# TensorE's order inside each turn of a chunked RWKV recurrence: the next block's inverse step put ahead of the state chain's step

## The chip, the cores and the metric

The kernel runs on one core of one Trainium2 chip. The metric is the device time of one execution in microseconds (us). The kernel before was timed three times: median 4484.01 us, from 4480.31 to 4486.97. The execution that left the profile took 4483.24 us.

A core has a matrix engine (TensorE, PE in the rows, its weight loads PEld), VectorE (DVE), ScalarE (ACT) and GpSimd (POOL), each with its own instruction queue which it works off in order, and SyncE (SP), which here issues the DMAs. They synchronise by semaphores. Matmuls write to PSUM, which has 8 banks; all operands here are float32.

## The reference

The program is three transformer blocks in sequence on 512 tokens of width 1024. The change touches one branch of the last layer, a bidirectional RWKV-7 recurrence with 16 heads of 64 channels:

```
def wkv7_step(state, inp):
    r, w, k, v, a, b = inp
    sa = jnp.einsum('...ij,...j->...i', state, a)
    state = (state * w[..., None, :] + sa[..., :, None] * b[..., None, :]
             + v[..., :, None] * k[..., None, :])
    y = jnp.einsum('...ij,...j->...i', state, r)
    return state, y
```

It is scanned over the 512 tokens forwards and backwards, with `-kk` (the normalised keys) as a and `kk * a` as b. Everything else (two FFNs, a gated delta rule, attention, an SSD and an HGRN scan, a second even layer, a Fourier branch) runs before or after this stage and is not touched.

## The kernel before

The scan is done in chunks. Two heads and one direction make one of 16 items i (ft = i // 2 is the pair of heads, d = i % 2 the direction), and the 512 tokens of an item are 4 chunks of 128. Within a chunk the recurrence becomes a triangular system: its inverse is built first (for all 4 chunks and both heads of the item at once, by doubling the block size from 2 to 64), and then the state is carried through the 4 chunks in sequence.

Four kinds of work are written as Python generators, for each engine one: `head` and `body` (what makes the decayed operands, the score matrices and their masks), `inverse` and `chain` (the state through the chunks); every second item there is also a `tail` (the normalisation of the output). `rw_rounds` (L401) runs 17 rounds r = -1..15. In round r an engine works at the chain of item r, the inverse of item r + 1, the body of item r + 2, the head of item r + 3 and, in even rounds, the tail of item r - 1. `together` (L205) takes one step (up to the next `yield`) of each generator in the order in which they are given, and starts again: one such pass is called a turn here. So the order of an engine's instructions within a turn is the order of the streams in the call of `together`, and nothing else reorders them. A round has some 14 turns; `chain` has three steps for each chunk n = 0..3, in turns 3n, 3n + 1 and 3n + 2.

What the steps issue on TensorE, with what they wait for:

- chain, turn 3n (n > 0): L3732, old state times keys ("rw rhs"); needs `rw s in`, VectorE's L3834 of the turn before.
- chain, turn 3n + 1: L3746, the inverse times the right side ("rw u", 4 small products, recorded as 8); needs VectorE's L3812 (which adds the own part to rhs).
- chain, turn 3n + 2: L3754 (own part of the state's update), L3756 (the update's part by the negated u; needs VectorE's L3817, which negates u, or for n = 0 ScalarE's L3786), L3762 (old state into the output) and L3764 (negated u into the output). VectorE then scales and adds the state (L3827, for n = 0 L3829) and masks it for the next chunk (L3834).
- inverse, even turns from 2: L938 ("inv x", 16 products), from turn 4 on also four transposes L923 ("inv t"); odd turns from 3: L954 ("inv y", 16 products). Turn 1 is four transposes L923 ("inv d"). x needs what VectorE's L1055 made of the y before, y needs what L1046 made of the x before and, from turn 5, ScalarE's copy L1010 of the transposes; the first x needs ScalarE's copy L1005 of turn 1.
- body and head: the scores L3459 (turns 3, 6, 8, 10), which VectorE masks in L3611, transposes L3442, L3428 (turn 5), L3374 (turn 0), L3499 and L3502.

VectorE's order within a turn is chain, inverse, body, head, tail, as it is on TensorE and ScalarE. PSUM banks are taken in turn from 7 (the eighth holds the chain's output), so an instruction may also wait until the tile that had its bank 7 takes before has been read.

Of the kernel before, what the change touches and what calls it, by code (L numbers as in the profile page):

```python
# [15 lines left out]
NT = 4  # L16
# [164 lines left out]
def run(steps):  # L181
    for _ in steps:
        pass
# [15 lines left out]
def behind(turns, steps):  # L199
    for _ in range(turns):  # L200
        yield
    yield from steps


def together(*streams):  # L205
    streams = list(streams)
    while streams:
        streams = [g for g in streams if next(g, "end") != "end"]
        yield
# [20 lines left out]
def assemble(nc, ctx, io, out):  # L230
# [25 lines left out]
    PS = [ctx.enter_context(nc.psum_tensor(f"ps{i}", [128, 512], F32))[:, :] for i in range(8)]  # L256
    banks, weights, sets = Turns(8), Turns(4), Turns(2)

    def mem(at_, tiles, width=TOK):
        return View(main[:, at_:at_ + tiles * width].rearrange("p (a b) -> p a b", b=width))  # L260
# [642 lines left out]
    def part128(a, i):  # L903
        return a[:, i * 128:(i + 1) * 128]
# [1182 lines left out]
    def ssd_order(d):  # L2087
        return list(range(NT)) if d == 0 else list(range(NT - 1, -1, -1))
# [1249 lines left out]
    RS_S, RS_S1 = mem(7232, 1, 128)(0), mem(7360, 2, 128)  # L3338
# [62 lines left out]
    def rw_rounds(e, head, body, inverse, chain, tail, aside):  # L3401


        none = iter(())
        run(together(rw_rest[e.name], behind(2, head(e, 1))))
        for r in range(-1, 16):
            ends = tail(e, r - 1) if r > 0 and r % 2 == 0 else none
            own = behind(0, chain(e, r)) if r >= 0 else none
            whole = inverse(e, r + 1) if r < 15 else none
            feeds = body(e, r + 2) if r < 14 else aside(e, r)  # L3410
            ahead = behind(5, head(e, r + 3)) if r < 13 else none
            run(together(*((own, whole, feeds, ahead, ends) if e.name == "act" else (own, whole, feeds, ahead, ends))))
        run(tail(e, 15))
        e.fence("rwkv")

# [302 lines left out]
    def pe_rw_chain(pe, i):  # L3718
        s, ft, d = sem["pe", "rwkv"], i // 2, i % 2
        FM, VK, MS, DT, RP = FMs[i % 3], VKs[i % 3], MSs[i % 6], DTs[i % 3], RPs[i % 3]  # L3720
        yb, before_y = banks.take("rw y", i, among=(0,))
        for hd in range(2):
            pe.wait_ge(*at("out", "rw ms", i, 4 * hd + 3))
        for n, c in enumerate(ssd_order(d)):
            s_ = slice(c * 128, (c + 1) * 128)
            rhs = RP[:, s_]
            if n:
                b, before = banks.take("rw rhs", i, n)
                if before:
                    pe.wait_ge(*at("out", *before))  # L3730
                pe.wait_ge(*at("rw s in", i, n))
                pe.mm(PS[b][:, 0:128], FM(0)[:, s_], RS_S1(n % 2), start=True, stop=True).then_inc(  # L3732
                    pe.inc(s, "mm", "rw rhs", i, n), 1)
                rhs = RS(0)
            yield
            b, before = banks.take("rw u", i, n)
            if before:
                pe.wait_ge(*at("out", *before))
            pe.wait_ge(*(at("out", "rw rhs", i, n) if n else at("out", "rw rhs own", i)))
            pe.wait_ge(*at("out", "inv t", 64, "early", "rw", i))  # L3740
            for k in range(2):
                pe.wait_ge(*at("out", "inv y", 64, k, "rw", i))
            pe.wait_ge(*at("rw dt zero", i))
            for hd in range(2):
                for h in HALF:
                    t = pe.mm(PS[b][h, 64 * hd:64 * hd + 64], part128(DT(hd), c)[:, h], rhs[:, 64 * hd:64 * hd + 64],  # L3746
                              start=True, stop=True)
            t.then_inc(pe.inc(s, "mm", "rw u", i, n), 1)
            yield
            if n < NT - 1:  # L3750
                b, before = banks.take("rw ds", i, n)
                if before:
                    pe.wait_ge(*at("out", *before))
                pe.mm(PS[b][:, 0:128], VK(1)[:, s_], VK(0)[:, s_], start=True, stop=False)  # L3754
                pe.wait_ge(*at("out", "rw u", i, n))
                pe.mm(PS[b][:, 0:128], VK(2)[:, s_], RS(1), start=False, stop=True).then_inc(  # L3756
                    pe.inc(s, "mm", "rw ds", i, n), 1)
            pe.wait_ge(*at("out", "rw u", i, n))
            if n == 0 and before_y:
                pe.wait_ge(*at("out", *before_y))  # L3760
            if n:
                pe.mm(PS[yb][:, s_], RS_S1(n % 2), FM(1)[:, s_], start=False, stop=False)  # L3762
            for hd in range(2):
                t = pe.mm(PS[yb][H2[hd], s_], RS(1)[:, 64 * hd:64 * hd + 64], MS[hd](3)[:, s_], start=n == 0,  # L3764
                          stop=n == NT - 1)
            t.then_inc(pe.inc(s, "mm", "rw y", i, n), 1)
            yield
# [138 lines left out]
    def pe_rwkv(pe):  # L3906
        input_here("lora")
        banks.only(range(1, 8))
        rw_rounds(pe, pe_rw_head, pe_rw_body, pe_rw_inverse, pe_rw_chain, pe_rw_tail, pe_rw_aside)
        banks.only(range(8))  # L3910

    def act_rwkv(a):
        after(a, "p")
        rw_rounds(a, act_rw_head, act_rw_body, act_rw_inverse, act_rw_chain, act_rw_tail, act_rw_aside)
# [14 lines left out]
    def dve_rwkv(v):  # L3929
        after(v, "p")  # L3930
        rw_rounds(v, dve_rw_head, dve_rw_body, dve_rw_inverse, dve_rw_chain, dve_rw_tail, dve_rw_aside)
# [203 lines left out]
```

## Time and profile before

| | |
|---|---|
| median of 3 runs | 4484.01 us |
| profiled execution, its own time | 4483.24 us |
| its span, first to last instruction | 4481.4 us |
| TensorE busy | 4331.1 us (97%) |
| VectorE busy | 2717.4 us (61%) |
| ScalarE, GpSimd busy | 793.4 us (18%), 171.5 us (4%) |
| mean granted TensorE clock | 0.990 |
| rounds 0 to 12 of the recurrence | 3745.7 to 4198.1 us |

Busy time is what the engine's instructions took, matmuls with their modelled ends, so 97% says that TensorE has few gaps and not that each of its cycles does work. The recurrence begins in the span at some 3717 us (round -1) and its chain ends at 4304 us. A round that has a tail is longer than one that has none. The granted clock is given as a share of 2.4 GHz, so 0.50 is the lower of the clock's two levels, 1.2 GHz. The time outside the span is 4483.24 - 4481.4 = 1.84 us.

### The profile page before, as it was taken

The page shows a single profiled execution, that of the slowest core. Times are in us where ns is not written, and L with a number is a line of the kernel's source. Part 1 is how long each engine was busy: PE and PEld are TensorE (multiplying, and loading weights), DVE is VectorE, ACT ScalarE, POOL GpSimd, SP SyncE. Part 2 cuts the span into 40 slices and gives each one's busy share as a digit, 9 for nine tenths or more (in the row PEclk, how much of TensorE's full clock was granted, in tenths as well). Part 3 has the DMA queues.
Part 4 walks back from the last instruction along what each step waited for, and adds up shares of the span by engine and source line. Part 5 has one row for each costly group of instructions (what it writes and reads, how often), then busy time and mean ns, then how long its engine had stood idle before and what let it go on. Part 6 is the DMA issues. An engine that isn't in the chain of part 4 may idle for free.

```text
span 4481.4 us, 68176 instructions
## 1 busy us (share of the span) xinstructions
PE 4331.1 (97%) x29692; PEld 3361.7 (75%) x29692; DVE 2717.4 (61%) x4765; ACT 793.4 (18%) x1434; POOL 171.5 (4%) x281
## 2 busy tenths in 40 slices
PE   9999999999999999999999999999999998999899
PEld 7887445577887888876755678887888787777767
DVE  6675878355555446676444556566556548888736
ACT  0001012221022000221222210000100104444311
POOL 0000000010000000000000000000000003222100
PEclk9999999999999999999999999999999999999999
DMA  7533454103222222111210122222222210000031
GB/s 256 169 115 64 68 75 69 29 2 85 94 94 66 94 85 87 59 57 38 66 48 29 55 69 93 85 85 76 94 73 88 81 47 12 2 3 3 12 103 48
DMA packets 284378, 311.52 MB, mean 70 GB/s; under 512 B 5168, under 2 KB 277936, under 8 KB 281008
## 3 DMA queue, kind: packets, MB, share of 16 engines
q1 hardware_dynamic: 284080, 307.16, 24.2%
q8 instruction: 234, 3.83, 0.4%
q14 instruction: 64, 0.52, 0.0%
HBM read 305.04 MB, written 2.10 MB: 69 GB/s over the span
## 4 chain that ended last, share of the span: by engine, by line
PE 90%; DVE 6%; ACT 2%; issue 1%; DMA 0%; SPq 0%; DVEq 0%; POOL 0%; ACTq 0%; POOLq 0%
PE ps L399 50%; PE ps L323 18%; PE ps L368 2%; PE ps L3459 1%; PE ps L2703 1%; PE ps L2489 1%; PE ps L938 1%; PE ps L923 1%; PE ps L954 1%; PE ps L540 1%; PE ps L2169 1%; PE ps L2158 1%; PE ps L3362 1%; PE ps L1383 1%; PE ps L754 0%
## 5 line engine op out<-in xcount | busy, mean ns | idle before, releaser
L399 PE MATMUL ps<-main 128*128 128x256 f32 x5888 | 1305.7, 379 | 0.0
L399 PEld LDWEIGHTS ps<-main 128*128 128x128 f32 x5888 | 1119.8, 190 | 151.0
L399 PE MATMUL ps<-main,w 128*128 128x256 f32 x4436 | 992.7, 380 | 3.5 <-DVE main L472 1.8
L399 PEld LDWEIGHTS ps<-main,w 128*128 128x128 f32 x4436 | 844.4, 191 | 122.9 <-issue 7.5
L323 PE MATMUL ps<-main,w 128*128 128x512 f32 (+1 forms) x1952 | 843.6, 587 | 12.7 <-DMA main<-in_xT 7.6
L323 PEld LDWEIGHTS ps<-main,w 128*128 128x128 f32 x1952 | 370.0, 193 | 423.7 <-issue 409.7
L491 DVE TENSOR_TENSOR main<-main,ps 128x512 f32<-128x512 f32 x189 | 130.0, 688 | 455.3 <-PE ps L399 454.9
L488 DVE TENSOR_TENSOR main<-main,ps 128x512 f32<-128x512 f32 x123 | 84.4, 686 | 233.8 <-PE ps L399 231.0
L438 ACT COPY main<-ps 128x256 f32<-128x256 f32 x123 | 45.7, 371 | 964.8 <-PE ps L399 962.4
L764 DVE SCALAR_TENSOR_TENSOR main<-main,params_sb 128x512 f32<-128x512 f32 x256 | 192.5, 752 | 9.1
L496 DVE TENSOR_TENSOR main<-main,ps 128x512 f32<-128x512 f32 x189 | 130.0, 688 | 86.9 <-PE ps L399 84.4
L448 DVE TENSOR_TENSOR main<-w 128x512 f32<-128x512 f32 (+2 forms) x189 | 127.6, 675 | 45.2 <-DMA w<-in_o_w_in 11.7
L451 DVE TENSOR_TENSOR main<-main,w 128x512 f32<-128x512 f32 (+2 forms) x189 | 128.9, 682 | 6.6
L453 DVE TENSOR_TENSOR main<-w,main 128x512 f32<-128x512 f32 (+2 forms) x189 | 128.9, 682 | 6.4
L449 DVE TENSOR_TENSOR main<-w 128x512 f32<-128x512 f32 (+2 forms) x189 | 127.6, 675 | 0.0
L3688 POOL MEMSET w<- 128x512 f32 x128 | 60.6, 525 | 1577.1 <-DVE tmp L3638 1282.6
L2544 DVE TENSOR_TENSOR main<-main 128x512 f32<-128x512 f32 x56 | 38.8, 692 | 127.7 <-PE ps L2489 125.1
L438 ACT COPY tmp<-ps 128x256 f32<-128x256 f32 x66 | 24.6, 372 | 498.9 <-PE ps L399 498.9
L488 DVE TENSOR_TENSOR main<-tmp,ps 128x512 f32<-128x512 f32 x66 | 45.3, 686 | 107.2 <-PE ps L399 106.3
L3611 DVE COPY_PREDICATED w<-consts_sb,ps 128x512 f32<-128x512 uint32 x128 | 85.9, 724 | 24.2 <-PE ps L3459 22.3
L368 PE MATMUL ps<-w,main 128*128 128x256 f32 (+1 forms) x512 | 99.1, 353 | 0.0
L368 PEld LDWEIGHTS ps<-w,main 128*128 128x128 f32 x512 | 87.5, 191 | 13.2 <-issue 3.8
(512 smaller groups left out, 4824.6 us busy)
## 6 DMA issues: line engine op xcount, KB each, us to landing
w<-in_w_in SPq DMA_DIRECT2D x58, 1024.0 KB, 8.1
w<-in_e_w_in SPq DMA_DIRECT2D x28, 1024.0 KB, 5.1
main<-in_ada_w SPq DMA_DIRECT2D x24, 1024.0 KB, 5.0
w<-in_ffn_wu SPq DMA_DIRECT2D x22, 1024.0 KB, 6.3
w<-in_ffn_wg SPq DMA_DIRECT2D x21, 1024.0 KB, 6.4
w<-in_o_w_in SPq DMA_DIRECT2D x20, 1024.0 KB, 5.5
w<-in_ffn_wd SPq DMA_DIRECT2D x16, 1024.0 KB, 5.1
w<-in_w_up SPq DMA_DIRECT2D x16, 1024.0 KB, 5.3
```

Of the source, the lines that this page charges most:

```text
L323: i = pe.mm(PS[b][:, 0:n], wv[:, k, f * 128:(f + 1) * 128], g.X(kg + k), start=kg + k == 0, stop=kg + k == g.nk - 1)
L368: i = pe.mm(PS[b][:, 0:m], g.X.ap[:, k, t * 128:(t + 1) * 128], wv[:, k, :], start=k == 0, stop=k == g.nk - 1)
L399: t = pe.mm(PS[b][:, 256 * half:256 * half + 256], weight[:, m, :], x(m), start=m == 0, stop=m == n - 1)
L448: v.tt(S[0], a21, a22, ADD).then_inc(v.inc(s, "sum 0", *step), 1)
L449: v.tt(S[2], a21, a11, SUB).then_inc(v.inc(s, "sum 2", *step), 1)
L451: v.tt(S[1], S[2], a22, ADD).then_inc(v.inc(s, "sum 1", *step), 1)
L453: v.tt(S[3], a12, S[1], SUB).then_inc(v.inc(s, "sums", *step), 1)
L488: v.tt(outer, two(first), b[1], ADD).then_inc(v.inc(s, "out", "seven", 1, *step), 1)
L491: v.tt(inner, two(c[3]), b[2], ADD).then_inc(v.inc(s, "most", *step), 1)
L496: v.tt(inner, inner, b[3], ADD).then_inc(v.inc(s, "out", "seven", 3, *step), 1)
L764: v.stt(out, src[:, j:j + TOK], w(j), out, MUL, ADD).then_inc(v.inc(s, "tap", j, *step), 1)
L3611: v.pick(c3(MS[hd](kind)), mid(const(mask), 4).bitcast(U32), c3(bank("rw ms", i, k))).then_inc(v.inc(s, "out", "rw ms", i, k), 1)
```

## The change

Two edits, both on TensorE alone. In `rw_rounds` TensorE's streams are now ordered inverse, chain, body, head, tail; the other engines keep chain, inverse, body, head, tail. In `pe_rw_chain` the product of the old state into the output (L3762 before, L3756 now) is issued before the wait for the negated u, and the two products that need the negated u come behind it. No instruction is added, taken away or resized; the later lines of the function move by one (L3756 is now L3759, L3764 is L3765).

```diff
             ahead = behind(5, head(e, r + 3)) if r < 13 else none
-            run(together(*((own, whole, feeds, ahead, ends) if e.name == "act" else (own, whole, feeds, ahead, ends))))
+            run(together(*((whole, own, feeds, ahead, ends) if e.name == "pe" else (own, whole, feeds, ahead, ends))))
         run(tail(e, 15))
...
                 pe.mm(PS[b][:, 0:128], VK(1)[:, s_], VK(0)[:, s_], start=True, stop=False)
+            if n:
+                pe.mm(PS[yb][:, s_], RS_S1(n % 2), FM(1)[:, s_], start=False, stop=False)
+            if n < NT - 1:
                 pe.wait_ge(*at("out", "rw u", i, n))
                 pe.mm(PS[b][:, 0:128], VK(2)[:, s_], RS(1), start=False, stop=True).then_inc(
                     pe.inc(s, "mm", "rw ds", i, n), 1)
             pe.wait_ge(*at("out", "rw u", i, n))
             if n == 0 and before_y:
                 pe.wait_ge(*at("out", *before_y))
-            if n:
-                pe.mm(PS[yb][:, s_], RS_S1(n % 2), FM(1)[:, s_], start=False, stop=False)
             for hd in range(2):
```

Here `own` is the chain, `whole` the inverse, `feeds` the body, `ahead` the head and `ends` the tail.

TensorE's queue in turns 1 to 3 of round 0, before. L3746 is the chain's u, L923 and L938 and L954 are the inverse's d, x and y, L3754, L3756 and L3764 the chain's turn 2, L3732 its turn 3:

```order
L3746 MATMUL ps<-main 64x64 [waits dve_rwkv,act_rwkv]
L3746 MATMUL ps<-main 64x64 x3
L923 MATMUL ps<-consts_sb,main 128x128 [waits pool_rwkv]
L923 MATMUL ps<-consts_sb,main 128x128 x3
L3754 MATMUL ps<-main 128x128
L3756 MATMUL ps<-main 128x128 [waits act_rwkv]
L3764 MATMUL ps<-w,main 64x128 x2
L938 MATMUL ps<-main,w 64x64 [waits act_rwkv]
L938 MATMUL ps<-main,w 64x64 x15
L3732 MATMUL ps<-main 128x128 [waits dve_rwkv]
L954 MATMUL ps<-main 64x64 [waits dve_rwkv]
L954 MATMUL ps<-main 64x64 x15
```

The same turns in the changed kernel:

```order
L923 MATMUL ps<-consts_sb,main 128x128 [waits pool_rwkv]
L923 MATMUL ps<-consts_sb,main 128x128 x3
L3746 MATMUL ps<-main 64x64 [waits dve_rwkv,act_rwkv]
L3746 MATMUL ps<-main 64x64 x3
L938 MATMUL ps<-main,w 64x64 [waits act_rwkv]
L938 MATMUL ps<-main,w 64x64 x15
L3754 MATMUL ps<-main 128x128
L3759 MATMUL ps<-main 128x128
L3765 MATMUL ps<-w,main 64x128 x2
L954 MATMUL ps<-main 64x64 [waits dve_rwkv]
L954 MATMUL ps<-main 64x64 x15
L3732 MATMUL ps<-main 128x128
```

The inverse's step has moved ahead of the chain's in each of the three turns, and the chain's products L3759 and L3732 have no wait of their own any more: the count of ScalarE's or VectorE's semaphore that they need has been reached when the inverse's step ahead of them may start.

TensorE's queue in turns 7 and 8 of round 0, before (L3442 is the body's):

```order
L3746 MATMUL ps<-main 64x64 [waits dve_rwkv,act_rwkv]
L3746 MATMUL ps<-main 64x64 x3
L954 MATMUL ps<-main 64x64 [waits act_rwkv,dve_rwkv]
L954 MATMUL ps<-main 64x64 x15
L3442 MATMUL ps<-consts_sb,w 128x128 x4
L3754 MATMUL ps<-main 128x128
L3756 MATMUL ps<-main 128x128 [waits dve_rwkv]
L3762 MATMUL ps<-main 128x128
L3764 MATMUL ps<-w,main 64x128 x2
L938 MATMUL ps<-main,w 64x64 [waits dve_rwkv]
L938 MATMUL ps<-main,w 64x64 x15
L923 MATMUL ps<-consts_sb,main 128x128 x4
```

And in the changed kernel:

```order
L954 MATMUL ps<-main 64x64 [waits dve_rwkv,act_rwkv]
L954 MATMUL ps<-main 64x64 x15
L3746 MATMUL ps<-main 64x64 x4
L3442 MATMUL ps<-consts_sb,w 128x128 x4
L938 MATMUL ps<-main,w 64x64 [waits dve_rwkv]
L938 MATMUL ps<-main,w 64x64 x15
L923 MATMUL ps<-consts_sb,main 128x128 x4
L3754 MATMUL ps<-main 128x128
L3756 MATMUL ps<-main 128x128
L3759 MATMUL ps<-main 128x128
L3765 MATMUL ps<-w,main 64x128 x2
```

L938 with its transposes stands ahead of the four products of the chain's turn 8, L954 ahead of L3746, and again only the inverse's first instruction of each turn waits.

## Rows read from the trace of the kernel before

**Rows 1.** Page, part 1: busy us (share of span) and instructions of each engine

```profile
PE 4331.1 (97%) x29692; PEld 3361.7 (75%) x29692; DVE 2717.4 (61%) x4765; ACT 793.4 (18%) x1434; POOL 171.5 (4%) x281
```

**Rows 2.** Windows: length, busy (instructions) by engine, PEclk, DMA share, GB/s

```profile
3745.70:4198.10 452.40, 416.07 (x8352) 335.34 (x8348) 370.88 (x940) 202.25 (x370) 114.79 (x182) 1.00 0.01 3
3988.20:4020.70 32.50, 30.40 (x632) 24.69 (x630) 27.54 (x70) 14.96 (x28) 9.29 (x14) 1.00 0.01 3
4020.70:4058.10 37.40, 33.79 (x660) 27.02 (x656) 29.70 (x76) 16.11 (x30) 8.29 (x14) 1.00 0.01 2
4234.00:4238.00 4.00, 2.49 (x70) 2.17 (x72) 2.94 (x9) 0.63 (x1) 0.00 (x0) 1.00 0.00 0
4239.00:4245.00 6.00, 5.18 (x59) 3.88 (x58) 3.37 (x12) 0.68 (x2) 0.00 (x0) 0.50 0.01 3
```

**Rows 3.** Waits of PE, rounds 0 to 12: total us, times, longest

```profile
PE ps L3756 <- DVE main L3817: 12.2, 19, 1.0
PE ps L3732 <- DVE main L3834: 9.1, 7, 1.3
PE ps L3459 <- DVE main L3851: 6.5, 6, 1.1
PE ps L3746 <- DVE main L3812: 3.4, 6, 0.6
PE ps L3746 <- DVE main L1067: 1.8, 6, 0.3
```

**Rows 4.** Timeline of PE, round 7, turns 1 to 3: start us, duration us

```profile
3989.08 0.40 PE L3746 MATMUL ps<-main 128*64 128x64 f32 x8
...
3990.82 0.69 PE L938 MATMUL ps<-main,w 64*64 64x64 f32 x32
3992.81 0.49 PE L3732 MATMUL ps<-main 128*128 128x128 f32 x2 [1.30 <-DVE main L3834]
...
3993.85 1.16 PE L3459 MATMUL ps<-main,w 64*128 64x128 f32 x16
```

**Rows 5.** Timeline of ACT and DVE, round 7, turns 1 and 2

```profile
3990.11 0.59 ACT L1005 COPY main<-ps 128x512 f32<-128x512 f32 x1 [0.30 <-PE ps L923]
...
3992.02 0.35 DVE L3829 TENSOR_SCALAR main<-ps,small 128x128 f32<-128x128 f32 x1
...
3992.67 0.48 DVE L1046 TENSOR_TENSOR main<-ps,consts_sb 128x128 f32<-128x128 f32 x2
```

**Rows 6.** Timeline of PE, round 7, turns 5 and 8

```profile
3996.88 0.39 PE L3754 MATMUL ps<-main 128*128 128x128 f32 x2
...
3998.01 0.69 PE L954 MATMUL ps<-main 64*64 64x64 f32 x32
3998.64 1.13 PE L3428 MATMUL ps<-main 64*128 64x512 f32 x4
...
4005.32 0.49 PE L3756 MATMUL ps<-main 128*128 128x128 f32 x2 [0.46 <-DVE main L3817]
...
4006.33 0.69 PE L938 MATMUL ps<-main,w 64*64 64x64 f32 x32
...
4007.54 1.16 PE L3459 MATMUL ps<-main,w 64*128 64x128 f32 x16
```

**Rows 7.** Timeline of DVE, round 7, turns 4 and 7

```profile
3996.28 0.28 DVE L3817 TENSOR_SCALAR main<-ps 128x128 f32<-128x128 f32 x1
...
3996.67 0.48 DVE L1046 TENSOR_TENSOR main<-ps,consts_sb 128x128 f32<-128x128 f32 x2
...
4004.97 0.29 DVE L3817 TENSOR_SCALAR main<-ps 128x128 f32<-128x128 f32 x1
...
4005.36 0.49 DVE L1055 TENSOR_TENSOR main<-main,ps 128x128 f32<-128x128 f32 x2
```

**Rows 8.** Timeline of DVE and PE, round 8 (with tail), turns 4 and 5

```profile
4033.74 0.47 DVE L1046 TENSOR_TENSOR main<-ps,consts_sb 128x128 f32<-128x128 f32 x2
...
4034.89 1.13 PE L3428 MATMUL ps<-main 64*128 64x512 f32 x4
```

## The prediction

> **What bounds the kernel now.** I read the page's first part first: TensorE is busy 97% of the span [rows 1], so the kernel is bound by TensorE's own work, and only what gaps there are can be won or lost by an order. Then I cut the span into windows. Rounds 0 to 12 of the recurrence take 452.4 us, with TensorE busy 416.1 of them, 36.3 us of gaps, and VectorE busy 370.9 [rows 2]. A round without tail takes 32.5 us with 2.1 us of gaps, a round with tail 37.4 with 3.6 [rows 2]. Nothing outside the recurrence is touched, so the whole effect is in 15 rounds (0 to 14) in which a chain and an inverse run side by side; round 15 has a chain but no inverse.
>
> The waits say what ends the gaps [rows 3]: TensorE waits for the chain's results from VectorE, 12.2 us in 19 waits for the negated u (L3817), 9.1 us in 7 for the masked state (L3834), 3.4 us for the right side (L3812). The inverse's results from L1046 and L1055 are not in this list at all. That is the picture to hold: TensorE asks first for the chain's result, VectorE makes first the chain's result, and while TensorE does the chain's step, VectorE makes the inverse's.
>
> **The change part by part.** Both edits leave each instruction as it is; only the place of waits moves. After it TensorE asks first for the inverse's result, but VectorE still makes the chain's first. So at a turn where TensorE arrives early it now waits until VectorE has done both, and then has both steps still before it. The price of a turn is worked out from round 7 (no tail), in which the timelines show all three places.
>
> Turn 8. TensorE's wait ends when L3817 is done, at 4005.32 [rows 6]. L1055 starts at 4005.36 and takes 0.49 [rows 7], so the inverse's L938 cannot start before some 4005.90. From there: L938 with its transposes, 4006.33 to 4007.54 = 1.21 [rows 6]; then the chain's four products, 1.13 by the same step in turn 5, where nothing held it (3996.88 to 3998.01) [rows 6]. The scores L3459 start at 4005.90 + 1.21 + 1.13 = 4008.24 instead of 4007.54 [rows 6]: +0.7. The product of the old state that is moved ahead of the wait gains nothing: the wait it was to fill (0.46 at this place) now lies ahead of the whole inverse step. VectorE's masks hang on those scores, so the delay is not given back there.
>
> Turn 5. In turn 4 TensorE did u first and then 1.21 of inverse; now u comes 1.21 later, ends at about 3996.6, and L3817 runs at 3996.7 instead of 3996.28 [rows 7]. L1046 behind it ends at 3997.15 + 0.4 = 3997.55, L954 starts at 3997.6 and takes 0.63 (3998.01 to 3998.64), then 1.13 of chain: L3428 starts at 3999.36 instead of 3998.64 [rows 6], +0.7. Here a wait arises where TensorE had none.
>
> Turns 1 to 3. Turn 1 is transposes and then u, so the negation on ScalarE and behind it the copy L1005, which the first L938 needs, come later: TensorE's pair ends at about 3990.1, L1005 runs from 3990.45 to 3991.05 (before: from 3990.11) [rows 5], L938 starts at 3991.1 instead of 3990.82 [rows 4]. The chain's update now stands behind L938, is done at about 3992.3, and L3829 starts 0.3 later than 3992.02 [rows 5]. L1046 ends at 3992.67 + 0.48 + 0.3 = 3993.45. Before, TensorE resumed at 3992.81 with the chain and had the scores at 3993.85 [rows 4]; now it resumes at 3993.5 with L954 (0.63), then L3732 (0.25), and has the scores at 3994.4: +0.5.
>
> The other turns I cost at nothing, because TensorE has a body step of about 1.1 us (scores, L3499) behind the chain's step, beside which VectorE finishes chain and inverse; if that cover were gone each would cost as turn 8. Sum of a round without tail: 0.5 + 0.7 + 0.7 = +1.9.
>
> With tail (round 8): turn 1 has a gain, since the transposes fill the 0.3 wait for L1067 (6 waits, 1.8 us [rows 3]); the wait for L3851, 6.5 us in 6 [rows 3], is VectorE's work and only shifts, so turns 1 to 3 cost +0.4. Turn 5: L1046 ends at 4034.21 [rows 8] + 0.4 = 4034.6, + 0.63 + 1.13 = 4036.4 instead of 4034.89 [rows 8], +1.5 in sum. In turns 6 to 8 VectorE's own tail work ends some of its waits less late, and the same addition as in turn 8 above leaves +1.3.
>
> The sum: 8 rounds without tail (0, 1, 3, 5, 7, 9, 11, 13) times 1.9 = 15.2; 6 rounds with tail (2 to 12) times 1.3 = 7.8; round 14, which has no body, nothing, with -1 to +3 as bounds, as its turns are near a serial loop either way. That is +23 us. The profiled execution took 4483.24, so 4506.2; the median shown is 0.8 above it, so 4507, and I say 4506.5.
>
> Bounds: if the slack elsewhere takes what each turn loses, and only turn 8 costs something (0.3, half of its price, in 14 rounds), +4; if each of the three turns costs 0.9 (L1046 or L1055 with L3820 and the chain step's lost head start), 14 x 2.7 = +38. I take the value worked out from the rows of the actual turns. The end of a matmul is modelled, so each step has perhaps 0.1 us in it.
>
> A clock that falls is not in this sum. The row shows it: in round 14, after 4 us with TensorE busy 2.49, the granted clock was 0.50 (1.2 GHz) for 6 us [rows 2]; in rounds 0 to 12 it stayed at 1.00 with 92% busy. The Trainium skill's page Perfetto Trace Analysis says under Matmul Optimizations that the matmul engine's speed follows its utilization and that matmuls should be issued back to back. The trace agrees with that rule for round 14 and not for the other rounds, whose waits of up to 1.3 us cost no clock. By the rule longer gaps speak against this change, and it is a rival below.
>
> **The rivals.**
>
> Faster: the inverse's step fills TensorE's waits for the chain. For it speak the 12.2 + 9.1 + 3.4 + 1.8 = 26.5 us of such waits [rows 3]; all of them gone gives 4457, half of them 4470. It needs the inverse's result to be there when the chain's is not. Against it speaks VectorE's order: L1046 or L1055 always stands behind the chain's instruction of the same turn [rows 5, 7]. The point that decides is turn 8: if L938 starts before 4005.3 of the old count, this rival is right. 8%.
>
> No change: the losses are there but go into slack, the waits for L3851 and L3812 (9.9 us in 12 [rows 3]) and VectorE's late work in the tail rounds. That leaves 0 to +9, say 4490. 14%.
>
> Slower by more: the clock falls in rounds in which it does not now. A fall costs half of the 5.18 us that TensorE was busy in the 6 us at 0.50 [rows 2], 2.6 us. In five rounds that is 13 us on top of 23: 4519; in all of them 4543. For it: turns 1 to 3 would have gaps of about 0.9 and 1.0 us around 1.4 us of work. 13%.
>
> The change not doing what it says can be ruled out in the program: the rows of the order show every chain step behind its inverse step and without a wait.
>
> **How the numbers follow.** Forecast, waits moved and lengthened, 4493 to 4515: 65%. With the rivals above, 8, 14 and 13%. A measurement of this kernel can tell 0.2%, 9 us, from no change: faster than 4475 is the first rival, 0.08; between 4475 and 4493 0.14; slower 0.78. The range from 4487 to 4524 leaves out the faster rival, the low part of the second and the high part of the third.
>
> **What would show it.** In the changed trace TensorE's waits for L3817, L3834 and L3812 should be next to gone and waits for L1046, L1055 and (turn 2) L1005 should stand in their place, some 55 us in rounds 0 to 12 where there were 36. A round without tail should take 34.4 us instead of 32.5, one with tail 38.7 instead of 37.4. TensorE's busy time should not change. If the rounds are not longer although those waits are there, the slack rival is right; if the granted clock in rounds 0 to 12 is under 1.00, the third. A time under 4487 makes the prediction wrong in its main step, that VectorE's order decides.

## The result, and the profile after

The changed kernel takes 4534.73 us (median of 4 runs, 4531.57 to 4538.81); the kernel before, in 4 runs, 4482.16. The ratio is 1.0119, with a 95% interval from 1.0102 to 1.0137: it is slower by 1.2%. The forecast was slower, by 23 us; the measured difference is 52.6 us, and 4534.73 is above the upper end of the range, 4524.

The page's first part, then windows of the changed kernel (length, busy us and instructions by engine, PEclk, DMA share, GB/s): rounds 0 to 12, round 7 (no tail), round 10 and round 8 (both with tail), a stretch of round 8 in which TensorE has its long wait, 3.4 us that begin 1.1 us behind it, and rounds 13 and 14:

```profile
PE 4345.8 (96%) x29692; PEld 3366.9 (74%) x29692; DVE 2718.6 (60%) x4765; ACT 792.0 (17%) x1434; POOL 168.8 (4%) x281
```

```profile
3743.20:4237.50 494.30, 431.80 (x8352) 344.34 (x8348) 372.82 (x940) 201.20 (x370) 112.42 (x182) 0.96 0.01 2
4008.60:4043.90 35.30, 30.70 (x637) 24.79 (x631) 28.05 (x70) 15.00 (x28) 8.96 (x14) 1.00 0.01 2
4120.80:4159.50 38.70, 33.52 (x661) 26.85 (x656) 29.78 (x76) 16.03 (x30) 8.29 (x14) 1.00 0.01 2
4043.90:4084.10 40.20, 35.03 (x660) 27.41 (x656) 29.81 (x76) 16.02 (x30) 8.28 (x14) 0.96 0.01 2
4053.90:4057.90 4.00, 1.72 (x28) 1.19 (x21) 1.52 (x6) 2.56 (x4) 3.53 (x5) 1.00 0.00 0
4059.00:4062.40 3.40, 3.40 (x13) 1.35 (x11) 3.00 (x7) 0.00 (x0) 0.00 (x0) 0.50 0.00 0
4237.50:4271.90 34.40, 30.07 (x621) 24.77 (x618) 25.10 (x59) 8.41 (x16) 8.95 (x14) 0.95 0.01 2
4271.90:4306.00 34.10, 26.25 (x490) 20.80 (x486) 17.85 (x53) 4.80 (x10) 0.00 (x0) 0.80 0.11 33
```

Read the first row against its counterpart of before [rows 2]. Rounds 0 to 12 take 494.3 us instead of 452.4, +41.9. Both windows hold the same 8352 records of TensorE, but its busy time is 431.8 instead of 416.1, +15.7: the same matmuls took longer, and the clock stands at 0.96 instead of 1.00. The rest, +26.2, is gaps (62.5 instead of 36.3). So there are two losses: TensorE waits more, and it works more slowly. The two rows of round 8 show how they hang together: 4 us in which TensorE is busy 1.72, and 1.1 us behind it 3.4 us at a clock of 0.50, that is 1.2 GHz.

A round's length runs from the start of the spreading products L3374 to the next. Before, every round without tail took 32.55 us and every one with tail 37.42, to 0.02. After, rounds 0, 1, 3 and 7 take 35.22 to 35.24 and round 10 takes 38.68, all at a full clock; the other eight are longer than their kind at full clock by 1.5 to 2.7 us, in each case with a fall of the clock inside. Summed: seven rounds of +2.68 and six of +1.26 are 26.3 us of waiting, and what is over in the eight rounds comes to 15.5 us. Two ways to read this trace, by busy time and by round lengths, give the same split.

The remaining difference lies behind round 12: rounds 13 and 14 take 8.4 us more. The same two rounds before:

```profile
4198.10:4229.00 30.90, 28.38 (x620) 23.51 (x618) 24.65 (x59) 8.41 (x16) 9.29 (x14) 1.00 0.01 3
4229.00:4258.20 29.20, 23.61 (x490) 18.91 (x488) 18.02 (x53) 4.92 (x11) 0.00 (x0) 0.88 0.13 38
```

In both the gaps have grown (by 1.8 and 2.3 us) and the busy time too (by 1.7 and 2.6), and the clock is lower. The way from the span's start to round 0 was 2.5 us shorter in this one execution, which makes 41.9 + 8.4 - 2.5 and some 0.6 behind the recurrence: the 48.4 us between the two spans.

TensorE's waits in rounds 0 to 12 (total us, times, longest), to be read against [rows 3]:

```profile
PE ps L954 <- DVE main L1046: 31.6, 26, 2.3
PE ps L938 <- DVE main L1055: 17.6, 14, 1.4
PE ps L938 <- ACT main L1005: 6.0, 7, 0.9
PE ps L3459 <- ACT main L3513: 3.7, 7, 0.6
PE ps L3459 <- DVE main L3852: 3.5, 6, 0.6
```

The waits for L3817, L3834 and L3812 are gone, as forecast, and 55.2 us of waits for the inverse stand in their place. The longest is in turn 5 of every round with tail; round 10 has it at a full clock:

```profile
4134.88 0.69 PE L954 MATMUL ps<-main 64*64 64x64 f32 x32 [2.30 <-DVE main L1046]
```

Round 7 on TensorE and ScalarE, the turns of [rows 4 to 6]; the round begins at 4008.66, before at 3988.16:

```profile
4011.58 0.69 PE L938 MATMUL ps<-main,w 64*64 64x64 f32 x32 [0.86 <-ACT main L1005]
...
4014.24 0.69 PE L954 MATMUL ps<-main 64*64 64x64 f32 x32 [0.95 <-DVE main L1046]
...
4015.28 1.16 PE L3459 MATMUL ps<-main,w 64*128 64x128 f32 x16
...
4019.51 0.69 PE L954 MATMUL ps<-main 64*64 64x64 f32 x32 [0.89 <-DVE main L1046]
...
4021.38 1.13 PE L3428 MATMUL ps<-main 64*128 64x512 f32 x4
...
4028.72 0.69 PE L938 MATMUL ps<-main,w 64*64 64x64 f32 x32 [1.30 <-DVE main L1055]
```

And VectorE in turns 2, 4 and 7, the instructions that end those waits [rows 5, 7]:

```profile
4013.61 0.48 DVE L1046 TENSOR_TENSOR main<-ps,consts_sb 128x128 f32<-128x128 f32 x2
...
4018.09 0.29 DVE L3818 TENSOR_SCALAR main<-ps 128x128 f32<-128x128 f32 x1 [0.26 <-PE ps L3746]
4018.30 0.57 DVE L3821 TENSOR_SCALAR main<-main,small 128x128 f32<-128x128 f32 x1
4018.78 0.47 DVE L1046 TENSOR_TENSOR main<-ps,consts_sb 128x128 f32<-128x128 f32 x2
...
4028.10 0.48 DVE L1055 TENSOR_TENSOR main<-main,ps 128x128 f32<-128x128 f32 x2
```

Counted from the round's start, the scores of turn 3 come at 6.62 instead of 5.69 (+0.93), L3428 at 12.72 instead of 10.48 (so turns 4 and 5 add 1.31), the scores of turn 8 at 22.32 instead of 19.38 (turns 6 to 8 add 0.70), and the round ends 2.68 later, so the turns from 9 on give 0.26 back. In round 10, with tail, the same three places come 0.26, 1.70 and 1.52 later than in the round 10 of before, and the round ends 1.26 later.

### The profile page after: what moved, and what is told of

It is laid out like the page before. It is cut to its first block, busy times and chain, and to the rows that moved or that the text cites. A ratio compares the mean times of both kernels' runs of the same rounds, so it can differ in the third digit from the quotient of the medians.

```text
span 4529.8 us, 68192 instructions
## 1 busy us (share of the span) xinstructions
PE 4345.8 (96%) x29692; PEld 3366.9 (74%) x29692; DVE 2718.6 (60%) x4765; ACT 792.0 (17%) x1434; POOL 168.8 (4%) x281
## 4 chain that ended last, share of the span: by engine, by line
PE 91%; DVE 6%; ACT 2%; issue 1%; DMA 0%; SPq 0%; DVEq 0%; POOL 0%; ACTq 0%; POOLq 0%
PE ps L399 49%; PE ps L323 18%; PE ps L368 2%; PE ps L3459 2%; PE ps L938 1%; PE ps L2703 1%; PE ps L2489 1%; PE ps L923 1%; PE ps L954 1%; PE ps L540 1%; PE ps L2169 1%; PE ps L2158 1%; PE ps L3374 1%; PE ps L1383 1%; PE ps L3362 0%
## 5 line engine op out<-in xcount | busy, mean ns | idle before, releaser
L954 PE MATMUL ps<-main 64*64 64x64 f32 x3200 | 72.3, 230 | 44.6 <-DVE main L1046 40.4
L954 PEld LDWEIGHTS ps<-main 64*64 64x64 f32 x3200 | 59.6, 139 | 65.1 <-DVE main L1046 51.8
```

What stands on the lines that cost most here:

```text
L954: t = pe.mm(PS[two[e][0]][HALF[q], 64 * n:64 * n + 64], E4[HALF[e], n, q, :], X4[HALF[e], n, q, :], start=True, stop=True)
```

## The experiments

Each is told with the interval of its ratio to the kernel before, or for single executions by its round lengths, which in those traces repeat to 0.02 us in rounds of a kind at a full clock.

### One edit at a time

`e1_order_only` has the first edit without the second:

```diff
-            if n:
-                pe.mm(PS[yb][:, s_], RS_S1(n % 2), FM(1)[:, s_], start=False, stop=False)
...
             pe.wait_ge(*at("out", "rw u", i, n))
...
+            if n:
+                pe.mm(PS[yb][:, s_], RS_S1(n % 2), FM(1)[:, s_], start=False, stop=False)
```

> The first edit alone: TensorE takes the inverse's step ahead of the chain's, the old state's product stays behind the wait for the negated u. Theory (VectorE makes the chain's result first, so TensorE's wait is moved behind both results; the longer gaps also let the clock fall): the product is no part of it, so the time is that of the changed kernel, 4529 to 4541 us, with falls of the clock in rounds 0 to 12 as there. Rival (the early product, which writes to the output's bank ahead of its wait, costs a good part): 4485 to 4515 us.

Measured: 4531.62 us, ratio 1.0123 (1.0103 to 1.0143). The whole loss is in the order of the streams. In its trace the clock falls too, in nine of the rounds 0 to 12 and not in the same ones.

`e2_product_only` has the second edit without the first:

```diff
-            run(together(*((whole, own, feeds, ahead, ends) if e.name == "pe" else (own, whole, feeds, ahead, ends))))
+            run(together(*((own, whole, feeds, ahead, ends) if e.name == "act" else (own, whole, feeds, ahead, ends))))
```

> The second edit alone: streams in the old order on TensorE, the old state's product ahead of the wait for the negated u. Theory: it fills up to 0.22 us of each of the 19 waits for L3817 in rounds 0 to 12, so 4477 to 4484 us, just under or at the kernel before, and the clock stays at 1.00 in those rounds. Rival (the product costs): over 4495 us.

Measured: 4477.67 us, ratio 0.9997 (0.9987 to 1.0007), no difference that the times can tell. The trace can tell it: rounds of 32.33 and 37.18 us instead of 32.55 and 37.42, at a full clock, some 3 us in rounds 0 to 12. The clock, expected at 1.00, fell once for 3.4 us, in round 6, which took 37.72. TensorE's wait for the negated u there (12.2 us before [rows 3]):

```profile
PE ps L3759 <- DVE main L3818: 7.6, 19, 0.8
```

The wait is 4.6 us shorter. The product's 0.22 us in 19 waits, as the theory had it, are 4.2 of them; the rest is in round 6, where slower work filled gaps.

### The order on all engines, and its mirror image

`e3_all_engines` gives VectorE and ScalarE TensorE's new order too:

```diff
-            run(together(*((whole, own, feeds, ahead, ends) if e.name == "pe" else (own, whole, feeds, ahead, ends))))
+            run(together(whole, own, feeds, ahead, ends))
```

> The changed kernel, but VectorE and ScalarE too take the inverse's step ahead of the chain's. Theory (it is the difference of the orders that costs, not the inverse being first): TensorE asks first for what VectorE makes first again, so the waits for L1046 and L1055 shrink to under 15 us in rounds 0 to 12, and the time is 4470 to 4495 us with a clock of 1.00 there. Rival (the state chain is what sets a turn's length, and whatever is put ahead of it costs, on any engine): 4515 us or more.

Measured: 4486.96 us, ratio 1.0017 (1.0007 to 1.0027). Rounds without tail take 32.82 us. Rounds with tail take 37.21 at a full clock, less than the 37.42 of before; four of the six are 38.75 to 40.93, with the clock down. Rounds 0 to 12 and TensorE's waits in them:

```profile
3740.50:4203.40 462.90, 424.25 (x8351) 339.63 (x8347) 369.13 (x939) 201.47 (x370) 119.29 (x182) 0.97 0.01 3
```

```profile
PE ps L938 <- DVE main L1055: 10.9, 13, 1.0
PE ps L954 <- DVE main L3818: 9.5, 6, 1.7
PE ps L3459 <- DVE main L3852: 7.2, 6, 1.2
PE ps L3459 <- ACT main L3513: 4.7, 7, 0.7
PE ps L954 <- DVE main L1046: 3.1, 7, 0.5
```

The gaps are 38.7 us, near the 36.3 of before and far from the 62.5 of the changed kernel. TensorE's queue, and with it the order in which it takes the PSUM banks, is here that of the changed kernel, so neither of them makes the loss. The inverse ahead of the chain costs little when the engine that answers has the same order. It is not free: this kernel has the early product too, and against the 32.33 and 37.18 us of `e2_product_only` the order on all three engines adds 0.49 us to a round without tail and 0.03 to one with tail, and the falls. The rival, that the state chain sets a turn's length whatever the others do, falls. The part of the expectation on the clock was wrong: it is 0.97, and 8.2 us of the 10.5 that these rounds are longer are busy time.

`e9_vector_only` is the mirror image, in the kernel of e2_product_only:

```diff
-            run(together(*((own, whole, feeds, ahead, ends) if e.name == "act" else (own, whole, feeds, ahead, ends))))
+            run(together(*((whole, own, feeds, ahead, ends) if e.name in ("dve", "act") else (own, whole, feeds, ahead, ends))))
```

> The mirror image: TensorE in the old order (chain, inverse; with the early product), VectorE and ScalarE take the inverse's step ahead of the chain's. Theory (what costs is that TensorE asks first for what VectorE makes second): TensorE now waits for the chain's results behind the inverse's, so it is slower than before too, 4495 to 4530 us, with longer waits for L3818 and L3835. Rival (only the inverse first on TensorE costs): 4478 to 4487 us.

Measured: 4517.39 us, ratio 1.0088 (1.0066 to 1.0111). Rounds 0 to 12, and the longest of TensorE's waits in them:

```profile
3755.80:4243.30 487.50, 442.15 (x8351) 359.57 (x8346) 370.77 (x939) 202.06 (x370) 116.35 (x182) 0.94 0.01 2
```

```profile
PE ps L3732 <- DVE main L3835: 23.4, 20, 1.4
PE ps L3759 <- DVE main L3818: 12.6, 19, 1.2
```

Against the 4477.67 us of `e2_product_only` the new order costs some 57 us on TensorE alone (the changed kernel), 40 on VectorE and ScalarE alone, and 9 on all three. In this kernel the larger part is the clock: busy time is 26 us more than before, gaps 9 us. A fall also hides waiting, because the slower work fills what would have been a gap, so this split is no measure of what the order alone would cost at a full clock. Two rounds with tail, 4 and 10, did keep the full clock: 37.55 and 37.57 us, 0.4 more than the 37.18 of `e2_product_only`. No round without tail did.

### Where in the round

A helper takes TensorE's inverse step first in some turns only; the early product is in all of them, so a round without tail has 32.33 us to start from:

```diff
+def together_by(first, own, whole, *rest):
+    streams, t = [own, whole, *rest], 0
+    while streams:
+        order = sorted(streams, key=lambda g: 0 if g is whole else 1) if t in first else streams
+        kept = [g for g in order if next(g, "end") != "end"]
+        streams = [g for g in streams if g in kept]
+        t += 1
+        yield
...
+            if e.name == "pe":
+                run(together_by((1, 2, 3), own, whole, feeds, ahead, ends))
```

`e6_turns_1_3`:

> The early product in all turns, TensorE's inverse step ahead in turns 1 to 3 alone. Theory (each early turn has its own price, and they add up to the +2.68 us of a full-clock round without tail): +0.9 us, so 33.2 us for a round without tail. The prediction's own price for these turns was +0.5 (32.8 us). Rival (the delay is made up by the slack behind it): 32.4 us.

Measured: 33.25 us, +0.92.

`e7_turns_4_5`:

> The early product in all turns, TensorE's inverse step ahead in turns 4 and 5 alone. Theory: +1.3 us, 33.6 us for a round without tail (VectorE's L1046, which ends the new wait, comes behind a later L3821 that runs beside GpSimd's L1029 and takes 0.57 instead of 0.28 us). The prediction's price was +0.7 (33.0 us). Rival (slack): 32.4 us.

Measured: 33.63 us, +1.30.

`e8_turns_6_8`:

> The early product in all turns, TensorE's inverse step ahead in turns 6 to 8 alone. Theory and prediction agree: +0.7 us, 33.0 us for a round without tail, from a wait of 1.3 us for L1055 in turn 8. Rival (slack): 32.4 us. If the three prices of this call, with the turns from 9 on, add up to well over or under +2.68, they do not act one by one.

Measured: 33.25 us, +0.92, where 0.7 was expected. The new wait takes also what the early product had filled (0.22 in a round without tail): counted against the kernel before it is the 0.70 read from the trace of after.

`e5_turns_9_on`:

> The early product of the second edit in all turns, and TensorE's inverse step ahead of the chain's in turns 9 to 13 of a round alone. In the changed kernel's round 7 these turns took 0.26 us less than before. Theory: TensorE has no wait there whose end would move, so a round without tail takes 32.07 us and one with tail 36.9 (before 32.55 and 37.42; the product alone 32.33 and 37.18), clock 1.00 in rounds 0 to 12, 4470 to 4480 us. Rival (the 0.26 came from slack that the earlier turns had left): rounds of 32.3 and 37.2 or longer.

Measured: 4473.2 us, ratio 0.9984 (0.9974 to 0.9993), in 11 runs: faster than the kernel before by 0.16%, and the lowest median here. Rounds without tail take 32.08 us, -0.25, rounds with tail 36.95; two of these take 37.5, with a fall of the clock for 3.4 us that was not expected. Over rounds 0 to 12 the order in these turns is worth some 3 us and the early product as much again. A window over one without tail, to be read against the round of [rows 2]:

```profile
3773.40:3805.40 32.00, 30.14 (x632) 24.73 (x630) 27.36 (x70) 14.93 (x28) 9.30 (x14) 1.00 0.01 3
```

The four prices are 0.92 + 1.30 + 0.92 - 0.25 = 2.89 us. The changed kernel's round, 35.23, is 2.90 over the 32.33 of the early product alone. In a round without tail each of the four groups of turns has its own price and they add up: no later turn makes good what an earlier one lost. In rounds with tail the parts are +0.28, +0.93 and -0.23 for e6, e8 and e5; e7 has a clock fall in each of them, so its part at full clock was not seen. There the parts do not add up: turns 6 to 8 cost 0.93 by themselves, but in the changed kernel, behind a turn 5 that comes 1.7 later, the scores of turn 8 come only 1.5 late.

### Why turns 4 and 5 cost so much

In the trace of after, L3821 (the state times the decay) takes 0.57 us in turn 4, and the same instruction in turn 7 of the round 0.28. `e11_pool_later` is e7 with a wait on GpSimd:

```diff
             for hd in range(2):
                 p.wait_ge(*at("out", "rw ms", i, 4 * hd))
+            if i > 1:
+                p.wait_ge(*at("rw s old", i - 2, 1))
```

> TensorE's inverse first in turns 4 and 5 alone (33.63 us for a round without tail), and GpSimd's L1029 waits until VectorE has done its state scaling (the tensor_scalar of 128x128 in turn 4). Theory: that instruction takes 0.28 instead of 0.57 us when L1029 does not run beside it, L1046 and so TensorE's wait end 0.3 earlier: 33.35 us. Rival (its length has another cause): 33.6 us.

The same place of round 0 in e7 and then in e11 (the instruction's line is L3834 in e7 and L3836 in e11, GpSimd's L1029 is L1039 in both):

```profile
3749.28 3.79 POOL L1039 TENSOR_TENSOR main<-w,consts_sb 64x256 f32<-64x256 f32 x4 [3.96 <-DVE w L3624]
...
3749.56 0.53 DVE L3834 TENSOR_SCALAR main<-main,small 128x128 f32<-128x128 f32 x1
```

```profile
3750.08 0.28 DVE L3836 TENSOR_SCALAR main<-main,small 128x128 f32<-128x128 f32 x1
...
3750.62 3.79 POOL L1039 TENSOR_TENSOR main<-w,consts_sb 64x256 f32<-64x256 f32 x4 [4.77 <-DVE main L1056]
```

The round takes 33.38 us instead of 33.63. So 0.25 of the 1.30 us is that VectorE's scaling had come to lie beside GpSimd's work: the old order had let most of it through ahead, in a round without tail.

### How much is the clock

`e4_filled` is the changed kernel with idle matmuls in the long waits:

```diff
+    FILL = {("y", 2): (2, 2), ("y", 4): (2, 5), ("x", 16): (3, 3)}
+
+    def pe_filled(pe, b, kind, m, name):
+        if name[0] == "rw" and 0 < name[1] < 15:
+            for _ in range(FILL.get((kind, m), (0, 0))[name[1] % 2]):
+                pe.mm(PS[b][:, 0:256], ident, consts[:, 0:256], start=True, stop=True)
...
+            pe_filled(pe, two[0][0], "y", m, name)
             pe.wait_ge(*at("out", "inv x", m, *name))
```

> The changed kernel with idle matmuls (128x256, identity times a constant, overwritten right after) in front of TensorE's three long waits of a round: 2 ahead of y in turn 3, 2 (with tail 5) ahead of y in turn 5, 3 ahead of x in turn 8, about as long as the waits before. Theory (some 16 us of the loss in rounds 0 to 12 is the clock falling in those gaps): the granted clock is 1.00 in rounds 0 to 12, and the time falls by 12 to 20 us to 4515 to 4523 us. Rival (the falls lie in time that is lost anyway, the waits alone are the loss): 4530 us or more, although the clock stays up.

Measured: 4521.25 us, ratio 1.0093 (1.0077 to 1.011). Rounds 0 to 12:

```profile
3744.50:4222.30 477.80, 464.20 (x8574) 372.23 (x8570) 373.90 (x940) 201.35 (x370) 112.50 (x182) 1.00 0.01 3
```

The clock is 1.00, all rounds of a kind are alike again (35.10 and 38.46; round 0 takes 36.4, because it has no tail and gets the five fillers of a round with tail), and the 13 rounds take 477.8 us instead of 494.3, 16.5 less, with 222 records of useless work more. That is the clock's share, measured without reading it off busy time, give or take 1 us: the rounds are 0.13 and 0.22 us shorter than those of the changed kernel at a full clock, and round 0 is 1.2 longer. What is left, 477.8 - 452.4 = 25.4 us, is the waiting.

`e10_late_kept` puts three such matmuls into round 14 of e5_turns_9_on, where the clock falls in the kernel before as well [rows 2]:

```diff
-        ("head", "qk", 0): 4, ("gdn first",): 4, ("rw kk", 1): 3}
+        ("head", "qk", 0): 4, ("gdn first",): 4, ("rw kk", 1): 3, ("rw var", 6): 3}
```

> The kernel with TensorE's inverse first in turns 9 to 13 alone, and three idle matmuls (128x256) in round 14 in the gap of 1.3 us ahead of the sums for the variance, after which the clock falls there. Theory: the clock stays at 1.00 in round 14 and the rounds' end comes some 2 us earlier, 4468 to 4476 us, below the kernel before by 0.1 to 0.3%. Rival (the gaps behind it bring the fall anyway): no difference from the kernel without them, 4473 us.

Measured: 4475.53 us, ratio 0.999 (0.9981 to 0.9999), not to be told from e5_turns_9_on. Two windows of 6 us in round 14, without and with the fillers (the second kernel's round begins 1.1 us sooner in the span):

```profile
4226.00:4232.00 6.00, 5.28 (x69) 4.53 (x72) 2.33 (x9) 0.94 (x3) 0.00 (x0) 0.72 0.01 3
```

```profile
4226.00:4232.00 6.00, 5.27 (x111) 4.48 (x109) 2.90 (x12) 0.69 (x2) 0.00 (x0) 1.00 0.01 3
```

The fall is gone, but from the start of round 13 to the chain's end it saves only 0.34 us (104.43 instead of 104.77), not 2. The rows show why. Without fillers, then with them (L312), from the sums for the variance (L3372) to the spreading products (L3384):

```profile
4226.39 1.02 PE L3372 MATMUL ps<-consts_sb,main 128*128 128x2 f32 x8 [1.32 <-ACT main L3810]
...
4232.50 1.09 PE L3384 MATMUL ps<-consts_sb,main 128*64 128x128 f32 x16
```

```profile
4224.53 1.56 PE L312 MATMUL ps<-consts_sb 128*128 128x256 f32 x6 [0.56 <-DVE main L3865]
4225.93 0.95 PE L3372 MATMUL ps<-consts_sb,main 128*128 128x2 f32 x8
...
4231.06 1.09 PE L3384 MATMUL ps<-consts_sb,main 128*64 128x128 f32 x16
```

This stretch takes 5.13 us instead of 6.11, so the fall of 3.4 us had cost 0.98. But the fillers are longer than the gap: counted from the start of round 13 (4188.62 and 4187.52), L3372 starts 0.64 later than without them, at 38.41 instead of 37.77. The fall in this round is also only half as long in `e5_turns_9_on` as in the kernel before (3.4 against 6.8 us).

## Why the prediction was wrong

The direction and the mechanism held: only the order costs (e1, e2), it costs because TensorE asks first for what VectorE makes second (e3, e9), and the waits moved to L1046, L1055 and L1005 with 55.2 us in rounds 0 to 12. That this meets the "some 55" is luck: the 36 beside it were all gaps, and counted like that there are now 62.5. The sum was 23 us and the change cost 52.6. By its steps:

- **The clock was made a rival of the waits, with 13%, and left out of the sum.** This is the step that failed. The falls are a consequence of the waits, so they belonged on top of the sum, not beside it. The price was set for 6 us at 0.50 (2.6 us); measured it is 15.5 us in eight rounds, 1.9 each, with 3.4 or 6.8 us at 0.50. The reason given, the gaps of turns 1 to 3, fits the falls that begin 5.2 to 5.5 us into rounds 5, 9 and 11; those of rounds 4, 8 and 12 begin 1.0 us behind the long wait of turn 5, which was not named as a reason. The prediction said that busy time would not change; it rose by 15.7 us in rounds 0 to 12, and filling the gaps took 16.5 away (e4). With the clock held up, the kernel takes 4521.25 us, inside the range. The rule of the Trainium skill that was weighed there (Perfetto Trace Analysis, Matmul Optimizations: the matmul engine scales its power with its utilization, which the prediction read as its speed) is borne out in these rounds, where before it was only in round 14: the clock is 0.96 with the longer gaps and 1.00 with the same gaps filled (e4).
- **Turns 1 to 3: +0.5 in the prediction, 0.92.** The start of L938 was estimated well (2.92 us after the round's start, by the sum 2.94). Behind it each hand-over came some 0.1 late: L1046 ended at 5.43 and L954 began at 5.58, and L3732 took 0.42 to the scores, not 0.25.
- **Turns 4 and 5: +0.7, 1.30.** Of the 0.6 too little, 0.25 is VectorE's scaling beside GpSimd (e11), 0.11 the chain's step, which took 1.24 behind L954 and not 1.13, and 0.2 the hand-over: L1046 ended at 4019.25 and L954 began at 4019.51, 0.26 behind it where the sum had 0.05.
- **Turns 6 to 8: +0.7, 0.70** against the kernel before. The estimate for turn 8 was right, and so was the statement that the early product gains nothing there.
- **The later turns: nothing, -0.26.** This is what the rival for a faster kernel was right about: with a body step behind and no wait to move, the new order is better. No run shows what makes it so. In round 7 TensorE has no wait in these turns in either trace; the way from L3362 to the transposes L3442 of turn 9 takes 2.79 us instead of 2.90, and that from the scores of turn 10 to L3499 2.40 instead of 2.51. In the traces a step of 64-wide products starts 0.1 sooner behind one of its kind (from L3765 to L3499 0.27, from L3764 to L954 0.37), but that was read, not tested.
- **Rounds with tail: +1.3, 1.26** at a full clock. Here two errors cancel: up to the scores of turn 8 the loss is 1.52 (by the sum 1.3), and the later turns, set at nothing, give 0.26 back. And behind their wait of 2.3 us in turn 5 begin five of the ten stretches at 0.50, three of them 1.0 us behind its end.
- **Rounds 13 and 14: +1.9, +8.4.** Round 14 had been set at nothing, since its turns "are near a serial loop either way". Its length went from some 29.8 to 34.7 us and round 13's from 30.9 to 34.4; the clock over round 14 is 0.80 instead of 0.88, so part is the clock again, part new waits of up to 1.1 us for L1046. Over both rounds the gaps have grown by 4.1 us and the busy time by 4.3; no run separates the two.

So of the 29.6 us that were missing, 15.5 are the clock in rounds 0 to 12, 6.5 are rounds 13 and 14, and 5.2 the turns that were priced too low (7 rounds of 0.78, less a little in those with tail). The 2.4 left are less than the two medians can tell.

## What to carry to other kernels

When two streams share a pair of engines, let both engines take them in the same order: what mattered here was much less which step is first (9 us) than that the engine that asks, asks first for what the other makes first (57 and 40 us). Reordering one side moves a wait behind both results, and each such place can be priced from the trace before: the end of the later result, plus the hand-over (0.1 to 0.26 us here, not nothing), plus all work that now stands behind the wait. The prices of places added up in rounds without tail and not in those with one, where more waits lie between them. If such a change lengthens the gaps of a TensorE that is at its full clock, add the falls to the price, they come with the waits. And an order need not be one for a whole round: taken only in the turns where no wait would move, it shortened each round by 0.25 us, and together with the early product it was worth 0.16% (e5_turns_9_on, 4473.2 us).

## What the runs showed of the hardware that was not expected

- In rounds without tail VectorE's 128x128 tensor_scalar from SBUF to SBUF takes 0.28 us alone and 0.53 to 0.57 beside GpSimd's tensor_tensor on 64x256 (e7, e11, after). The same operation reading PSUM just ahead of it (L3818) took 0.29 although it too lay beside that instruction (after, round 7).
- The clock fell 1.1 us behind 4 us with TensorE busy 1.72. Falls came in eight of thirteen rounds that otherwise are alike in their kind to 0.02 us: rounds 4 and 10 have the same waits (0.95, 0.6 and 2.30 us in turns 3 and 5) and the same 1.72 us, and only round 4 has a fall. Whether a fall comes cannot be read from one round.
- What 3.4 us at 0.50 cost differed with the waits behind them: 1.5 to 1.6 us in rounds 4, 5, 8, 9 and 12 of the changed kernel, 0.98 in round 14 (e5 against e10), and 0.5 in round 6 of e2 and rounds 2 and 8 of e5, where TensorE has a wait for VectorE behind them anyway.
